# Spreading TensorE's narrow products and transposes among wide projections, and splitting the last h tiles earlier, in a hybrid mLSTM and differential-attention block

## The reference

```python
xn = rmsnorm(x, pre_g)
proj = xn @ w_in                       # q, k, v, gates, o, z of both branches, merge gates
# mLSTM, 4 heads, two directions, state C (128 x 256) and normaliser n (128) per chunk:
den = w_inter * einsum(q, n) + sum(s)
C_new = decay * C + einsum(wk, k, v)
n_new = decay * n + einsum(wk, k)      # the normaliser products
h_a = sigmoid(m_o) * rmsnorm(h) * silu(m_z)
# differential attention, 8 heads
o = softmax(q0 k0) v - lam * softmax(q1 k1) v
h_b = rmsnorm(o) * silu(a_z)
g = sigmoid(g_merge + b_merge)
y = g_a * (h_a @ w_branch_m) + g_b * (h_b @ w_branch_a)
out = x + rmsnorm(y @ w_out, post_g)
```

## Time and profile before

| | us |
|---|---|
| median of 3 runs | 1657.06 (1656.74 to 1658.99) |
| profiled execution, its own time | 1660.44 |
| profiled execution, span from first to last instruction | 1658.4 |
| TensorE busy | 1600.7 (97%) |
| VectorE busy | 985.6 (59%) |
| ScalarE busy | 831.5 (50%) |
| mean granted TensorE clock | 0.989 |

### The profile page before, as it was taken

The page is one execution under the profiler, slowest core; times in us unless marked ns, Lnnn a source line. Parts: engine busy times, 40 slices in busy tenths (PEclk is TensorE's granted clock), DMA queues, the critical chain, the costliest instruction groups (busy, mean ns, idle before and its releaser), DMA issues.

```text
span 1658.4 us, 23808 instructions
## 1 busy us (share of the span) xinstructions
PE 1600.7 (97%) x8311; PEld 1338.9 (81%) x8311; DVE 985.6 (59%) x1607; ACT 831.5 (50%) x1474; POOL 542.7 (33%) x589
## 2 busy tenths in 40 slices
PE   6999999999999999999999999999999998999998
PEld 5788888888888878787777778787878887888898
DVE  6803774765665667777777777777776112334313
ACT  5314654654655654646464646555555234555312
POOL 4242152252161255151414233333310333333560
PEclk8999999999999999999999999999999999999999
DMA  5131021121121231212121212111211535432432
GB/s 164 34 121 39 26 88 39 55 72 38 51 74 29 66 87 29 58 32 58 32 57 32 57 32 57 32 44 32 53 60 32 181 114 165 152 92 86 127 102 102
DMA packets 130138, 116.08 MB, mean 70 GB/s; under 512 B 5210, under 2 KB 116379, under 8 KB 129060
## 3 DMA queue, kind: packets, MB, share of 16 engines
q1 hardware_dynamic: 125476, 102.78, 21.8%
q10 hardware_dynamic: 4608, 12.58, 2.0%
HBM read 85.96 MB, written 21.00 MB: 64 GB/s over the span
## 4 chain that ended last, share of the span: by engine, by line
PE 70%; DVE 10%; ACT 9%; issue 8%; DMA 2%; DVEq 0%; ACTq 0%; SPq 0%
PE ps L696 50%; PE ps L704 6%; PE ps L1002 6%; PE ps L908 2%; PE ps L900 2%; ACT aT_split L1903 2%; DVE aT_split L1437 2%; DMA k_stack<-k_stack 2%; DVE negmax L1432 2%; ACT probs L1898 1%; PE ps L785 1%; DVE state_f L1293 1%; ACT num L1801 1%; ACT w_split L1599 1%; PE ps L723 1%
## 5 line engine op out<-in xcount | busy, mean ns | idle before, releaser
L696 PE MATMUL ps<-xn_split,w_split 128*128 128x512 f32 x4224 | 1012.0, 396 | 0.4 <-DVE gate_cols L1198 0.4
L696 PEld LDWEIGHTS ps<-xn_split,w_split 128*128 128x128 f32 x4224 | 788.3, 189 | 166.6 <-DVE gate_cols L1198 0.6
L590 POOL TENSOR_TENSOR w_split<-w_raw,w_split 128x256 fp32r<-128x256 f32 x384 | 327.7, 884 | 956.9 <-ACT w_split L1599 956.3
L1898 ACT ACTIVATE probs<-ps,negmax 128x1024 f32<-128x1024 f32 x128 | 143.0, 1117 | 129.6 <-DVE negmax L1432 129.6
L1432 DVE TENSOR_REDUCE negmax<-ps 128x1 f32<-128x1024 f32 x128 | 150.0, 1212 | 2.4 <-PE ps L900 2.4
L1437 DVE TENSOR_TENSOR aT_split<-ps,aT_split 128x512 fp32r<-128x512 f32 x128 | 88.4, 691 | 100.8 <-ACT aT_split L1903 99.9
L900 PE MATMUL ps<-k_stack,q_stack 128*128 128x512 f32 x512 | 133.7, 403 | 2.8 <-DMA k_stack<-k_stack 2.7
L900 PEld LDWEIGHTS ps<-k_stack,q_stack 128*128 128x128 f32 x512 | 91.4, 188 | 20.9 <-issue 3.3
L704 PEld LDWEIGHTS ps<-aT_split,va_split 128*128 128x128 f32 x768 | 95.1, 190 | 10.6 <-issue 7.1
L704 PE MATMUL ps<-aT_split,va_split 128*128 128x256 f32 x768 | 98.8, 285 | 2.5 <-DVE aT_split L1437 1.9
L1599 ACT ACTIVATE w_split<-w_raw 128x1024 fp32r<-128x1024 f32 x94 | 98.9, 1052 | 0.2
(11 more groups left out here) (247 smaller groups left out, 1773.8 us busy)
## 6 DMA issues: line engine op xcount, KB each, us to landing
w_raw<-in_w_in SPq DMA_DIRECT2D x80, 512.0 KB, 3.9
k_stack<-k_stack SPq DMA_DIRECT2D x16, 512.0 KB, 4.2
qk_f<-spill_g SPq DMA_DIRECT2D x16, 512.0 KB, 3.6
spill_g<-qk_f ACTq DMA_DIRECT2D x12, 512.0 KB, 2.6
w_argument<-m_rows SPq DMA_DIRECT2D x8, 512.0 KB, 5.3
spill_m<-hT_f ACTq DMA_DIRECT2D x16, 256.0 KB, 2.2
spill_a<-o_out SPq DMA_DIRECT2D x32, 128.0 KB, 1.8
h_split<-spill_m SPq DMA_DIRECT2D x8, 512.0 KB, 5.0
```

Source lines behind the costliest of these rows:

```text
L590: lo = pool.tensor_tensor(wsp[b][:, 1, ks_], raw[b][:, ks_], wsp[b][:, 0, ks_].bitcast(F32), ALU.subtract)
L696: mm = pe.matmul(ps[:, half, :], wsp[b][:, wl, k, :], moving[:, xl, k, cols], start=(k == 0 and n == 0), stop=(k == KT - 1 and n == 2))
L1898: act.activation(pr[:, c], ps[:, 2 + 2 * c:4 + 2 * c, :].rearrange("p b k -> p (b k)"), ACT.Exp, bias=nmax[:, b, c:c + 1], accum_out=den[: ...
```

## The change

In the preparation, the decays and the four groups of eight transposes are moved from in front of tile 6 to five places within it: after 3 and after 6 of the 8 k-tiles of each half and between the halves. In every mLSTM head the normaliser products are no longer made in front of step 0 but two chunks at a time, in steps t = 0..3, between intra and upd. In the gate stage ACT makes the high part of h tile n-1 between the two reads of gate tile n, and for the last gate tile the high parts of h tiles 6 and 7 both, between its two reads.

```diff
-            pe.wait_ge(prep_act, prep_act_at("decay"))
-            for m in range(MH):
-                for r in range(2):
-                    at = 256 + 2 * NC * m + NC * r
-                    mm = pe.matmul(ps[:, 7, at:at + NC], pick[:, r, m, :], r_dec[:], start=True, stop=True)
-            mm.then_inc(prep_pe, 1)
-
-            pe.wait_ge(prep_act, prep_act_at("w_k"))
-            for q, row in enumerate((r_i, r_winter, r_t, r_wk)):
+            def gate_decays():
+                pe.wait_ge(prep_act, prep_act_at("decay"))
...
+            def gate_columns(q):
+                pe.wait_ge(prep_act, prep_act_at("w_k"))
+                row = (r_i, r_winter, r_t, r_wk)[q]
                 for c in range(NC):
                     mm = pe.transpose(ps[:, 2 + q, c * ROWS:(c + 1) * ROWS], row[:, c * P:(c + 1) * P],
                                       ident[0:ROWS, 0:ROWS])
-            mm.then_inc(prep_pe, 1)
-            for half in range(2):
-                proj_half(0, 0, 0, 6, half)
+                return mm
+
+            proj_half(0, 0, 0, 6, 0, end=3)
+            gate_decays()
+            proj_half(0, 0, 0, 6, 0, begin=3, end=6)
+            gate_columns(0)
+            proj_half(0, 0, 0, 6, 0, begin=6)
+            gate_columns(1)
+            proj_half(0, 0, 0, 6, 1, end=3)
+            gate_columns(2)
+            proj_half(0, 0, 0, 6, 1, begin=3, end=6)
+            gate_columns(3).then_inc(prep_pe, 1)
+            proj_half(0, 0, 0, 6, 1, begin=6)
...
-            def n_updates(h):
-
-                pe.wait_ge(hcols.sem, hcols.after(h, 0))
-                for c in range(NC):
+            def n_updates(t):
+
+                for c in (t, NC - 1 - t):
                     at = MV + 4 + 2 * c
                     pe.matmul(ps[:, 7, at:at + 2], kseq[:, c], hc[:, c:16 - c:15 - 2 * c, Q_WK], start=True, stop=True)
...
                 mm.then_inc(intra_done.sem, 1)
+                if t < NC // 2:
+                    n_updates(t)
                 if t < NC - 1:
...
                 m_scores(h, 0)
-                n_updates(h)
+                pe.wait_ge(hcols.sem, hcols.after(h, 0))
...
-                    for half in range(2):
-                        read_gate(G_G, 2, c, j, half, 8 + j + 2 * c, qkf, fbias[:, j:j + 1])
-                    h_high(0, 2 * c + j)
+                    n = 2 * c + j
+                    read_gate(G_G, 2, c, j, 0, 8 + n, qkf, fbias[:, j:j + 1])
+                    if n > 0:
+                        h_high(0, n - 1)
+                    if n == KT - 1:
+                        h_high(0, n)
+                    read_gate(G_G, 2, c, j, 1, 8 + n, qkf, fbias[:, j:j + 1])
```

More of the change, by code:

```diff
@@ L757, in _ @@
                 proj_half(0, 0, 0, j, 1)
-            pe.wait_ge(prep_act, prep_act_at("decay"))
-            for m in range(MH):
-                for r in range(2):
-                    at = 256 + 2 * NC * m + NC * r
-                    mm = pe.matmul(ps[:, 7, at:at + NC], pick[:, r, m, :], r_dec[:], start=True, stop=True)
-            mm.then_inc(prep_pe, 1)
-            pe.wait_ge(prep_act, prep_act_at("w_k"))
-            for q, row in enumerate((r_i, r_winter, r_t, r_wk)):
+            def gate_decays():
+                pe.wait_ge(prep_act, prep_act_at("decay"))
+                for m in range(MH):
+                    for r in range(2):
+                        at = 256 + 2 * NC * m + NC * r
+                        mm = pe.matmul(ps[:, 7, at:at + NC], pick[:, r, m, :], r_dec[:], start=True, stop=True)
+                mm.then_inc(prep_pe, 1)
+            def gate_columns(q):
+                pe.wait_ge(prep_act, prep_act_at("w_k"))
+                row = (r_i, r_winter, r_t, r_wk)[q]
                 for c in range(NC):
```

## The result

| | before | after |
|---|---|---|
| median of 5 runs, us | 1657.15 (1656.74 to 1659.22) | 1650.52 (1647.17 to 1651.64) |
| profiled execution, its own time | 1660.44 | 1651.64 |
| span | 1658.4 | 1649.6 |
| mean granted clock | 0.989 | 0.996 |

The ratio is 0.9949 with a 95% interval of 0.9936 to 0.9962: faster by 0.5%. The prediction had 12.3 us, 1644.8; the medians differ by 6.6 and the profiled executions by 8.8. The median after lies 0.5 us above the forecast range; the ratio times the median of before, 1648.7, lies inside it. The five runs after fall into two groups, near 1651 and near 1647.5.

The account below looks back on a forecast made before the run. TensorE, busy 97% of the span, bounds the kernel; its idle time and lower clock can be won. Preparation 2.82 + heads 2.54 + handover 6.94 = 12.3 us, 1657.06 - 12.3 = 1644.8, range 1642.5 to 1650.0.

Parts of the forecast that it names:

- the preparation: From first decay to reversing product: 15.21 us instead of 18.03, a gain of 2.82.
- I take it that the clock holds: Tile 6: spread decays and transposes leave the clock up; otherwise this part is worth -0.4 us.
- the price of a piece: Tile 6: each return from narrow to wide work costs 0.08 us, five returns 0.40.
- the prediction's sentence on it: TensorE weight loads: by the skill's rule breaks would cost nothing, making the sum 13.3 us and the time 1643.7.
- the comparison for the clock: Tile 6: longest narrow stretch 1.81 us of decays, against 2.37 us of scores and normaliser products in the heads.
- the clock falls in spite of the spreading: Rival in the preparation: the clock still falls, that part is worth -0.4, gain 9.1, time 1648.0; chance 0.08.
- the slower rival: mLSTM heads: normaliser pieces lengthen narrow runs to 3.2 us; up to 16 falls of 1.59, about +16, 1673; chance 0.02.
- The heads: mLSTM heads: 3.18 us of lower clock saved, less 0.64 for 16 new pieces, a gain of 2.54.
- The rival that called the falls chance: mLSTM heads: if timed runs have no clock falls there, the gain is 9.1, time 1648.0; chance 0.16.
- The handover: Gate stage to branch product: 4.64 us of idle time and 2.3 of lower clock go, a gain of 6.94.
- The rival of a bank not free: First branch tiles: a late attention tile load makes TensorE wait for bank 0; gain 7.7, time 1649.4; chance 0.12.
- the 3.4 us between profiled execution and median: Whole kernel: profiled time is 3.4 us above the median; difference carried over unchanged, 1657.06 - 12.3 = 1644.8.

Follow-up runs that it names:

- two blocks: Changed kernel, with decays in one block before tile 6 and all 32 transposes between its halves: 1645.06, ratio 0.9921; repeated, 1645.01, ratio 0.9926.
- the gate part alone: Kernel before, with only the decays and transposes moved to five places within tile 6: 1659.2 against 1658.05, ratio 1.0007.
- the transposes late: Changed kernel, decays unmoved, the four groups of transposes one k-tile apart late in half 1 of tile 6: 1647.41, ratio 0.9934.
- twelve pieces: Changed kernel, with decays in four pieces and transposes in eight groups of four, one behind each of 12 k-tiles: 1648.67 against 1657.71, ratio 0.9937.
- eight pieces: Changed kernel, with decays in four pieces one k-tile apart and transposes still in groups of eight: 1647.6, ratio 0.9934.
- without the gate part: Changed kernel, with decays and transposes put back as one block in front of tile 6: 1647.2 against 1658.05, ratio 0.9933.
- the handover alone: Kernel before, with only the early high parts of h tiles in the gate stage: 1652.69 against 1658.05, ratio 0.9963.
- the first four experiments: The change without its tile 6 edit, then each of its three edits alone on the kernel before: 1647.2, 1659.2, 1652.69, 1654.51 against 1658.05.

## Why the prediction was half right

Direction and two of three parts were right; the whole was 6.6 us by the medians and 8.8 by the profile instead of 12.3, because of the preparation.

**The step that failed** is "I take it that the clock holds", with the arithmetic behind it. Predicted 15.21 us and a gain of 2.82; the new order took 20.80, 17.88 and 19.28 in three traces, with a fall in each. The old took 18.03, 16.59, 16.59 and 15.01, with a fall in three of four. Three things went wrong in it.

First, the price of a piece. I took 0.08 from two lengths of a wide half, one behind narrow products of 128 rows and one behind wide ones, and counted only the return. Against the one block at 15.01, the excess without a fall is 0.31 for one more piece (two blocks, 15.32), 2.22 for seven (17.23) and 3.53 for eleven (18.54): 0.31, 0.32 and 0.32 each. In the two blocks, 0.21 of it lies in the wide work: its halves take 5.71 in front of the 36-row transposes and 5.61 in front of the 128-row reversing product, against 5.50 within a long run. So the return costs 0.11, near to my 0.08, and the way into 36-row work another 0.10. The last 0.10 lies in the narrow work itself (1.88 + 2.12 against 3.90 in one block). So the five pieces of the change cost 4 x 0.32 = 1.3 more than one, and the stretch would be 16.3 with the clock at full speed, not 15.2. The Trainium skill (TensorE: Matmul & The Clock Gate, Part 2, step 1) says that loads are pulled ahead of matmuls in flight where the row groups do not conflict or where they go to the background weight buffer; the prediction's sentence on it left out this condition. No row shows whether it is met for 36-row weights between 128-row ones, but the rows here, 0.36 us of an idle loader in front of each piece, do not agree with a free break.

Second, the comparison for the clock. I held 1.81 us of decays against 2.37 us of scores and normaliser products, and called the shorter one safe. The decays, alone among wide matmuls, stand in front of a fall in all four traces in which they lie after three k-tiles of tile 6 (the change twice, the gate part alone, the transposes late). With the decays in four pieces, or as a block of their own in front of the tile, four traces (twelve pieces, eight pieces, two blocks twice) have none. That an undivided block of decays in front of tile 6 does not bring the clock down while one inside it does is seen, not explained. TensorE itself gets the same order in both, up to the first transposes: wide matmuls of tile 5 on, 16 decay instructions, 24 wide matmuls. With the transposes late only nine more wide matmuls stand in front, so that the decays start at 109.85 instead of 108.29. What differs is when they come, and that it is the moment that decides, and not the place, is a rival that no run excludes; two traces are few.

Third, what holds the clock down. From tile 6 to the first branch product the twelve traces hold 15 stretches at the low clock. In ten of them TensorE ran nothing but wide matmuls: tile 6 with the transposes late, in the gate part alone (where the clock is back at 115.7, just before the first group), without the gate part and with the handover alone; five heads; and the branch product in the version with the normaliser products alone. All ten lasted 3.4 us. In the other five narrow work or idle time fell inside: the transposes in tile 6 before (6.8 us), in the change (10.2) and in its second trace (6.8), and TensorE's wait in front of the branch product in two traces (6.8 each). There was room for more with wide work alone: without the gate part 8 us of it still followed when the clock came back.

In tile 6 the fall cost 1.6 us for 3.4 at the low clock (17.88 and 17.90 less 16.3; 16.59 less 15.01), 3.0 for 6.8 (19.28 less 16.3, 18.03 less 15.01) and 4.5 for 10.2 (20.80 less 16.3). So groups of transposes that left the clock at 1.00 where it had not fallen (decays in four pieces) stood in all three long stretches of tile 6 and in none of the four short ones. The version with the transposes late moves them out of the fall's reach, but it is one trace, and in the other versions it was chance how near to a group the clock fell. So the cause is strongly suggested, not isolated. In the changed kernel it was 6.8 us where the clock fell at 113.7 and 10.2 where it fell at 114.2. The rival "the clock falls in spite of the spreading" had a chance of 0.08 and a time of 1648.0; it is what came, and its price of -0.4 for this part should have been about -1.3 (16.3 plus a fall of 3.0, 19.3, against the 18.03 of that trace).

The prediction's price of the slower rival has a slip in it: 25.4 - 12.3 - 3.2 is not +16. The falls in the heads that are not saved have to be added back, 25.4 - 12.3 + 3.2 = 16.3, which is the number that it used.

**The heads** were right, with the size off by 1.4: 3.94 measured, 2.54 predicted. The falls gave 3.2 as reckoned. The pieces cost nothing instead of 0.64, and heads without a fall became 0.15 to 0.2 shorter. Part of that is the wait for pt_split, which went from 6.2 us over four heads to 5.7. The chain of VectorE and ScalarE took up the later upd without a new wait of TensorE, as argued. The rival that called the falls chance was excluded by the count of heads (5 of 12 against 0 of 36), and so was the slower one: no window in the steps is below 1.00.

**The handover** was right in each step: 6.88 against 6.94. The low parts took 1.2 us each with POOL idle, as the row for xn_split had suggested, and the margin was 0.84 us against 0.9, reckoned as the prediction did with 0.34 between VectorE's end and TensorE's start (1374.16 - 1372.98 - 0.34). ACT's first read of the branch product came at 1383.63, 9.5 us after TensorE's start (predicted 9.35). The high part of the first attention tile kept its place behind the gate tiles: it came 1.98 us sooner than before, the reads of the last gate tile 1.93. The second half's read came in time. The lower clock behind the idle time cost 2.06 by the two traces, not 2.3. The rival of a bank not free was not seen in any of the traces. The timed gain of this edit alone, 5.4 (3.8 to 8.3), is less sharp than the trace's.

The difference between the profiled gain of 8.8 and the timed one of 6.6 is within what the executions of either kernel differ by: 5.1 us over the 20 runs of before that the first four experiments shared, 4.5 over five of the changed one. The prediction carried the 3.4 us between profiled execution and median over unchanged; this one execution before happened to hold the costlier falls (18.03 for the stretch, two heads) and the latest second half of tile 0 (48.99), and so overstated what was to be won.

## What to carry to other kernels

Narrow work between wide matmuls is not free to scatter. Before it is spread, price one piece, on its way in, in itself and on the way back (here 0.3 us in all when its weights have 36 rows, nothing measurable when they have 128 and the neighbours are short), and compare with the fall of the clock that it is to prevent (1.6 us or more, in some executions). One cut in the middle did better than four: side by side, two blocks gave 1645.0 and five pieces 1649.6. One block gave 1647.2 in another set of runs; that two blocks beat it is not clear of the noise.

Idle time at a handover is the safer find, where the last item could be made sooner and only the written order of an engine keeps it back. It costs twice, here 4.6 us as idle time and 1.7 to 2.1 as the lower clock behind it; it stood in all three traces without the edit and in none of the nine with it.

Where the clock falls in one execution and not in the next, read the same stretch in several traces before putting a number on it.

## What the hardware showed that I had not expected

Eight decay products (16 instructions, 1.88 us) inside a run of wide matmuls were followed by the lower clock in four traces of four, although at least 60 us of wide work stood directly in front of them. The same eight products in front of the tile, with 32 transposes behind (3.9 us in all), left it at 1.00 in one trace of four, and with 24 wide matmuls behind in two of two.

From tile 6 to the first branch product the stretches at the low clock came in three lengths only, 3.4, 6.8 and 10.2 us, ten times the shortest, four times the middle one and once the longest, and the shortest every time when nothing but wide matmuls ran in it.

A piece of work with 36-row weights cost 0.31 to 0.32 us on top of its own time, whether it held 4 instructions or 32, while a piece of four instructions with 128-row weights among products of 256 columns cost nothing measurable (0.44 against a quarter of 1.75). No run changes the number of rows alone, so that the rows make the difference is suggested by the idle loader (0.36 us in front of 36-row work, none in front of the 128-row transposes), not shown.
